# Second halves of a two-layer encoder kernel: attention steps four units apart, attends eight units behind, bias rows a pair ahead

## The reference

```python
def hybrid_layer(x, w_in, a_group_w, a_scale, b_sinks, c_rel_bias, w_out, ln_gain, ln_bias):
    h = jnp.einsum('bsd,de->bse', x, w_in)
    a_v, a_gate, b_q, b_k, b_v, b_gate, c_q, c_k, c_v, c_gate = jnp.split(h, _split_points(), axis=-1)
    a_out = pool_mixer(a_v, a_group_w, a_scale) * jax.nn.silu(a_gate)
    b_out = swa_sink_attention(b_q, b_k, b_v, b_sinks) * jax.nn.silu(b_gate)
    c_out = chunk_relbias_attention(c_q, c_k, c_v, c_rel_bias) * jax.nn.silu(c_gate)
    mix = jnp.concatenate([a_out, b_out, c_out], axis=-1)
    y = jnp.einsum('bse,ed->bsd', mix, w_out)
    return _layer_norm(DEEPNORM_ALPHA * x + y, ln_gain, ln_bias)
```

## Time and profile before

| what | before |
|---|---|
| median of three runs | 2870.41 us (2867.22 to 2871.13) |
| the profiled execution: time, span | 2874.22 us, 2872.4 us |
| PE busy | 2780.0 us, 97% of the span |
| DVE, ACT, POOL busy | 64%, 44%, 45% |
| low half of a unit on POOL (L1418), mean | 1410 ns |
| mean granted clock of TensorE | 0.989 |

### The profile page before, as it was taken

The page is one execution under the profiler, slowest core; times in us unless marked ns, Lnnn a source line. Parts: engine busy times, 40 slices in busy tenths (PEclk is TensorE's granted clock), DMA queues, the critical chain, the costliest instruction groups (busy, mean ns, idle before and its releaser), DMA issues.

```text
span 2872.4 us, 41015 instructions
## 1 busy us (share of the span) xinstructions
PE 2780.0 (97%) x12836; PEld 2313.4 (81%) x12836; DVE 1836.3 (64%) x2950; ACT 1267.9 (44%) x2612; POOL 1294.0 (45%) x927
## 2 busy tenths in 40 slices
PE   8888999999999999999999999999999999999998
PEld 7777888888877787888888888888888877788886
DVE  4555568732687777873157776796146778778624
ACT  4433456532344445553234444654234444456521
POOL 4334444444544444444454444444444444444441
PEclk9999999999999999999999999999999999999999
DMA  6555533255678873325567775323567667532442
GB/s 203 144 146 155 161 92 88 85 176 179 199 214 220 227 195 90 92 85 169 184 193 200 208 202 157 89 85 121 161 213 206 188 190 202 150 97 82 128 161 103
DMA packets 470981, 448.04 MB, mean 156 GB/s; under 512 B 257664, under 2 KB 308896, under 8 KB 467104
## 3 DMA queue, kind: packets, MB, share of 16 engines
q1 hardware_dynamic: 467024, 430.19, 52.1%
q10 hardware_dynamic: 3792, 15.73, 1.4%
HBM read 358.69 MB, written 90.27 MB: 156 GB/s over the span
## 4 chain that ended last, share of the span: by engine, by line
PE 78%; DVE 11%; DMA 6%; issue 2%; ACT 2%; SPq 1%; POOL 0%; ACTq 0%; POOLq 0%; DVEq 0%
PE acc L698 53%; PE sc L698 15%; PE pv L698 9%; DMA pt_raw<-c_prob_scratch 3%; DVE pt L1450 2%; DMA c_prob_scratch<-prob 2%; PE sc L767 1%; DVE mixl L1450 1%; DVE nmax L1504 1%; ACT pt L1030 1%; DVE c_att L1483 1%; DVE prob L1513 0%; DVE sc L1502 0%; DVE c_low L1480 0%; DVE b_keys L1450 0%
## 5 line engine op out<-in xcount | busy, mean ns | idle before, releaser
L1418 POOL TENSOR_TENSOR wl<-raw,wh 128x512 fp32r<-128x512 f32 x920 | 1293.2, 1410 | 1535.2 <-ACT wh L1030 1524.2
L1030 ACT ACTIVATE wh<-raw 128x512 fp32r<-128x512 f32 x920 | 574.0, 629 | 1071.7 <-PE acc L698 770.1
L698 PE MATMUL acc<-xh,wh 128*128 128x512 f32 x2624 | 1035.3, 395 | 7.5 <-DVE mixl L1450 4.1
L698 PE MATMUL acc<-xl,wh 128*128 128x512 f32 x2624 | 1027.5, 392 | 0.0
L698 PE MATMUL acc<-xh,wl 128*128 128x512 f32 x2624 | 1026.7, 391 | 0.0
L698 PEld LDWEIGHTS acc<-xh,wh 128*128 128x128 f32 x2624 | 496.8, 189 | 105.9 <-DVE mixl L1450 4.5
L698 PEld LDWEIGHTS acc<-xh,wl 128*128 128x128 f32 x2624 | 495.6, 189 | 106.6
L698 PEld LDWEIGHTS acc<-xl,wh 128*128 128x128 f32 x2624 | 496.5, 189 | 95.1
L1450 DVE TENSOR_TENSOR xl<-prob,xh 128x512 f32 x48 | 55.6, 1159 | 237.7 <-ACT xh L1030 237.7
L698 PE MATMUL sc<-wh,mixh 128*128 128x512 f32 x496 | 193.5, 390 | 0.1
L698 PE MATMUL sc<-wl,mixh 128*128 128x512 f32 x496 | 193.0, 389 | 0.0
(11 more groups left out here) (214 smaller groups left out, 3642.0 us busy)
## 6 DMA issues: line engine op xcount, KB each, us to landing
raw<-in_wall SPq DMA_DIRECT2D x920, 256.0 KB, 2.8
c_prob_scratch<-prob SPq DMA_DIRECT2D x128, 160.0 KB, 3.0
pt_raw<-c_prob_scratch SPq DMA_DIRECT2D x32, 640.0 KB, 5.1
res_scratch<-res ACTq DMA_DIRECT2D x12, 1024.0 KB, 4.3
res<-res_scratch SPq DMA_DIRECT2D x12, 1024.0 KB, 6.1
res<-in_x SPq DMA_DIRECT2D x8, 1024.0 KB, 6.9
x_scratch<-res SPq DMA_DIRECT2D x8, 1024.0 KB, 5.1
x_t_scratch<-turned SPq DMA_DIRECT2D x128, 64.0 KB, 2.7
```

The lines of the kernel that those rows point to most:

```text
L698: return nc.tensor.matmul(o, lhsT, rhs, start=start, stop=stop)
L1030: return nc.scalar.activation(o, i, ACT.Copy, scale=scale)
L1418: nc.gpsimd.tensor_tensor(wl[:, s, :], raw[:, s, :], wh[:, s, :].bitcast(F32), ALU.subtract).then_inc(w_lo, 1)
```

## The change

- Second halves get an order of their own on PE, ACT and DVE (`second_half`): scores after units 16, 20, 24 and 28, attends after 24, 28, 32 and 36 (24 is unit 0 of the next pair). SP stores and loads c_prob at u 26/28, 30/32, 34/36 and 38/40.
- In second halves the rows for gain and bias go to `brope[:, 0, :]` and `av` (`ln_rows`) and not to `prob`; they are loaded at s 22, store_ln and store_turned stand at u 27 to 31.
- `bias_rows` of pair p + 1 is issued by ACT in pair p behind slot 12, once bias_in of pair p has come; pair 0's stays.
- In it 0, `low_keys` stands ahead of the bias rows on DVE.
- Tails of all steps: B's second query tile is projected into `q_bank` (sc[1]); the B keys are split ahead of the last product of C; the transposed B values go to `vals` and not to `tmp`; b_scores waits for c_fold and not for the product. Pair 3 folds into `c_atts` and `c_lows` of other buffers.

```diff
-STORE_AT = (26, 29, 32, 36)
-LOAD_AT = (28, 31, 35, 38)
-ROPE_AT = C_PAIRS * 24 + 11
+STORE_AT = ((26, 29, 32, 36), (26, 30, 34, 38))
+LOAD_AT = ((28, 31, 35, 38), (28, 32, 36, 40))
+LAST_STORE_AT = (STORE_AT[0], (26, 30, 34, 36))
+LAST_LOAD_AT = (LOAD_AT[0], (28, 32, 35, 38))
+ROPE_AT = (C_PAIRS * 24 + 11, C_PAIRS * 24 + 12)
...
+        c_atts = [c_att] * (C_PAIRS - 1) + [av[:, 0:HALF]]
+        c_lows = [c_low] * (C_PAIRS - 1) + [res[:, 0, :]]
...
+        def ln_rows(it, slot):
+
+            if half(it + 1):
+                return (brope[:, 0, :], av[:, 0:HALF])[slot]
+            return prob[:, slot, 0:512]
...
+                if half(it + 1):
+                    sp.wait_ge(bias_ok, n + (C_PAIRS * (it + 1) + 2))
+                    sp.wait_ge(ay_ok, n + (C_PAIRS * (it + 1) + 1))
+                elif n:
                     sp.wait_ge(cp_out, 64 * c_step(it + 1, n, 0))
...
-                    if s == 10 and half(it):
+                    if s == (12 if half(it) else 10) and half(it):
...
-                    if s == 13 and it:
+                    if s == (22 if half(it) else 13) and it:
                         load_gain_bias(it - 1, p)
...
+                        if half(it) and u == q * U_C + 27:
+                            store_ln(it - 1, q)
+                        for t in range(QT):
+                            if half(it) and turns(it) and u == q * U_C + (27, 29, 29, 31)[t]:
+                                store_turned(it - 1, q, t)
...
-                pe.wait_ge(prod_ok, MIXES * it + 2 * C_PAIRS + 2)
+                pe.wait_ge(c_fold, 4 * C_PAIRS * (it + 1) + 2)
...
+                def second_half(p):
+                    def quarter(s, bank, **how):
+                        project(it, p * U_C + s, s % 4, acc[bank][:, :], s % RING, **how)
+
+                    if p:
+                        c_scores(it, p - 1, 2)
+                        c_attend(it, p - 1, 0)
+                    for s in range(1, 4):
+                        quarter(s, 0)
+                    pe.wait_ge(gate_ok, p * 2 + (MIXES * it + 1))
+                    pe.wait_ge(out_free, 16 * it + 8)
+                    quarter(4, 1)
+                    if p:
+                        c_scores(it, p - 1, 3)
+                        c_attend(it, p - 1, 1)
...
+                        if u in (KV0, KV0 + 2):
+                            c_scores(it, last, 2 + (u - KV0) // 2)
+                        if u in (KV0, KV0 + 4, KV0 + 7, B0 + 2):
+                            c_attend(it, last, (KV0, KV0 + 4, KV0 + 7, B0 + 2).index(u))
...
-                    def bias_rows():
+                    def bias_rows(q):
                         act.wait_ge(rel_out, 16)
+                        if q:
+                            act.wait_ge(bias_in, 16 * q)
...
                     slot(12)
+                    if it == 0 and p + 1 < C_PAIRS:
+                        bias_rows(p + 1)
...
```

The tail of DVE:

```diff
                 rotate(it, 1, KV0 + 7, 1, 1.0)
                 c_lo(it, p, 3)
-                c_add(it, p, 3)
-                c_tail_product(p, C_PAIRS * (it + 1))
-                dv.wait_ge(prod_ok, MIXES * it + 2 * C_PAIRS + 2)
...
-                mix_lo(nb + 2 * C_PAIRS, p + MIX_C)
                 if half(it):
                     dv.wait_ge(hist_mv, layer(it) + 1)
                 dv.wait_ge(qh_ok, ROTS * it + 2)
                 keys_lo([k[:, HD:] for k in bkl], s0[:, 0:HALF], [k[:, HD:] for k in bk]).then_inc(bq_ok, 1)
-                rotate(it, 2, B0 + 3, 0)
+                c_add(it, p, 3)
+                rotate(it, 2, B0 + 3, 1, source=q_bank)
+                c_tail_product(p, C_PAIRS * (it + 1))
+                dv.wait_ge(prod_ok, MIXES * it + 2 * C_PAIRS + 2)
                 rotated_query(ROTS * it + 3, 1)
+                dv.wait_ge(w_used, unit(it, B0 + 7) + (1 + RING))
+                V.transpose(vals, v_bank).then_inc(vt_ok, 1)
+                mix_lo(nb + 2 * C_PAIRS, p + MIX_C)
```

More of the change, by code:

```diff
@@ L600, in pair_end @@
                 def pair_end(p):
-                    if it:
+                    if it and not half(it):
                         if turns(it):
@@ L862, in _ @@
+                step(KV0)
+                for s in range(1, 4):
+                    project(it, KV0 + s, s, acc[0][:, :], s)
+                    step(KV0 + s)
                 pe.wait_ge(gate_ok, MIXES * it + 2 * C_PAIRS + 1)
@@ L1244, in _ @@
                 for p in range(C_PAIRS):
-                    pair(p, it + p == 0)
+                    if half(it):
+                        second_half(p)
+                    else:
+                        pair(p, it + p == 0)
                 last = C_PAIRS - 1
[L1248 to L1266, removed]
@@ L1655, in c_tail_product, with coefficients @@
                     dv.wait_ge(c_fold, c_step(it, p, 3) + 1 + 2)
-                    attention_product(p * 2 + (MIXES * it + 2), values)
-                for p in range(C_PAIRS):
-                    section(total)
-                    if p:
-                        c_max(it, p - 1, 3)
-                        c_lo(it, p - 1, 1)
+                    attention_product(p, p * 2 + (MIXES * it + 2), values)
+                def coefficients(p):
                     V.tensor_copy(coef1[:], coef[:, ds(p, 1), :].rearrange("p o n -> p (o n)"))
@@ L1670, in _, with pooling @@
                         V_(V.memset(av[:, 0:16], 0.0))
-                    if p:
-                        c_normalise(it, p - 1, 3)
-                        c_add(it, p - 1, 1)
-                        c_lo(it, p - 1, 2)
+                def pooling(p):
                     dv.wait_ge(av_ok, p + (pc + 1))
@@ L1756, in _ @@
                 p = C_PAIRS - 1
-                c_max(it, p, 3)
-                c_lo(it, p, 1)
-                c_normalise(it, p, 3)
-                c_add(it, p, 1)
-                c_lo(it, p, 2)
+                if half(it):
+                    for k in (*bk, *bkl):
+                        last = V.tensor_copy(k[:, 0:HD], k[:, HALF:HALF + HD])
+                    last.then_inc(hist_mv, 1)
+                    c_max(it, p, 2)
+                    c_add(it, p, 0)
+                    c_normalise(it, p, 2)
+                    c_lo(it, p, 1)
+                    c_max(it, p, 3)
+                    mix_lo(nb + 2 * C_PAIRS - 1, p + MIX_A)
+                    c_add(it, p, 1)
+                    c_normalise(it, p, 3)
+                    c_lo(it, p, 2)
+                else:
+                    c_max(it, p, 3)
+                    c_lo(it, p, 1)
+                    c_normalise(it, p, 3)
+                    c_add(it, p, 1)
+                    c_lo(it, p, 2)
                 dv.wait_ge(rope_in, 32 * (it + 1))
```

380 lines of the change are left out of this document (300 added, 80 removed).

## The result

The changed kernel takes **2930.3 us** (median of four runs, 2926.7 to 2932.1), the kernel before, run beside it, 2868.8 (2866.5 to 2871.1): ratio 1.0213, 95% interval 1.0195 to 1.0231, so 61.5 us slower. Predicted were 2848 us, and 2812 to 2871 as the range.

The account below looks back on a forecast made before the run. TensorE was taken as the bound, busy 97%, so only its idle time and slow clock could be won. Terms -27.5 + 6.6 - 4.8 + 0.9 + 2 = -22.8 us on 2874.2 gave 2851.4, as a median 2848; range 2812 to 2871.

Parts of the forecast that it names:

- bias rows: In it 0, issuing them a pair ahead removes three waits near 8 us and their slow clock: -27.5 us.
- attend 0, it 1, four pairs: PE's c_attend of step 0: SP stands at u 27 for turned rows, so load 0 is late, 3.3 us a pair.
- attend 1, it 1, three pairs: PE's c_attend of step 1: load_ln (1 MB) goes just ahead of its load, 0.4 us a pair.
- attend 3, it 1, three pairs: PE's c_attend of step 3: chain from attend 1's end 25.8 us, PE has 23.3, so 2.5 us late a pair.
- attend 3, it 3, three pairs: The same step 3 chain in the pairs of it 3: 2.5 us late a pair, bounds 0.3 and 6.7.
- tails: attend 2: PE's c_attend of step 2 in the tails of second halves: no wait counted, 0 us.
- tails: attend 3: Second halves' tails: c_lo 3 stands behind rotations and the rope load behind store 3, about 4.0 us late, twice.
- second halves, slow clock: Fewer waits, but seven above 3 us in it 1 and four in the tails: one more slow stretch, +2 us.
- Rival (2): Bias transfer only moves, holding history store and weights; PE waits 8 us in three pairs again: 2880 us, chance 0.08.
- the sizing of the second halves' waits: Late-step sums against the old waits: it 1 21.9 against 15.3, it 3 9.5 against 14.3, tails 12.6 against 11.7.
- Rival (3): Second halves' loads behind 1 MB take the upper bound, 6.7 us for 2.5, six times: 25 us more, 2873, chance 0.13.
- Rival (1): Second halves do as the spacing says: 29.6 us of waits and four slow stretches go, 2809 us, chance 0.20.

Follow-up runs that it names:

- e1: The kernel before with only the bias rows of pair p + 1 issued behind slot 12 of pair p: 2845.4 us, ratio 0.9913.
- e2: The changed kernel with the bias rows issued where the kernel before issues them: 2952.0 us, ratio 1.0283.
- e3: The changed kernel with SP's LN store at u 29 and turned rows at u 29, 29, 31, 31 in second halves: 2916.2 us, ratio 1.0156.
- e6: The changed kernel with second halves' load_ln moved to s 9 and history keys to s 13, behind loads 1 and 2 of c_prob: 2906.8 us, ratio 1.0126.
- e9: e8 with the second halves' turned rows moved on DVE from ahead of c_lo 0 to behind it: 2870.1 us, ratio 0.9996.
- e4: The changed kernel with c_normalise of step 3 ahead of c_lo of step 2 on DVE in second halves: 2882.4 us, ratio 1.0045.
- e8: The changed kernel with e3, e4, e6, ACT's splits of B0+4 and B0+5 ahead of the last mix_hi, and rope rows fetched at slot 11: 2841.1 us.
- e11: e8 with the wide spacing in it 3 alone, it 1 back in the order of the kernel before: 2832.6 us, ratio 0.9872.
- e10: e9 with the bias rows of the pair ahead issued behind slot 17 and not slot 12: 2874.2 us, ratio 1.0015.

## Why the prediction was wrong

By its own steps, predicted against the profile after:

| step | predicted | measured |
|---|---|---|
| bias rows | -27.5 | -26.0 (it 0's stretch); -25.2 alone (e1) |
| attend 0, it 1, four pairs | 3.3 each | 6.2, 7.0, 6.5, 5.7 |
| attend 1, it 1, three pairs | 0.4 each | 2.2, 2.0, 2.0 |
| attend 3, it 1, three pairs | 2.5 each | 5.8, 4.8, 5.8 |
| attend 3, it 3, three pairs | 2.5 each | 6.3, 6.8, 6.6 |
| attend 0, it 3, four pairs | 0.5 each | 0.5, 2.2, 2.0, 1.9 |
| tails: attend 2 | 0 | 3.6 twice |
| tails: attend 3 | 4.0 twice | 6.5, 6.1 |
| tails: B0+7 | 2.3 twice | 2.1, 1.7 |
| second halves, slow clock | +2 | +28.0 (20.7 and 7.3) |

**The bias rows** were right in mechanism and size, 23.7 us of waits against 23.8 of idle time (34.9 to 11.1); PE was 2.2 us less busy in it 0, where 5.8 were counted for the slow clock. A new stretch at 0.50 at 10.8 us (3.4 us) took back 1.7 of it, the rest stays open. Rival (2), the transfer that only moves, is out: e1 and e2. What pair 0 does (the wait stays, for `wl`) came as said.

**The step that failed is the sizing of the second halves' waits (+6.6 and -4.8, and +0.9 for the tails), and with it the clock term (+2).** The runs showed 42.4 us of waits in it 1 where it summed 21.9, 27.4 in it 3 where it summed 9.5, and 28.0 us of slow clock. Every wait that came was one that the prediction named, but for attend 2 in the tails and most of attend 1: it named the places and, in all, gave them 40% of their price. The waits came to 97.1 us (42.4 + 15.8 + 27.4 + 11.5) where it had summed 21.9 + 9.5 + 8 for attend 3 in the tails. Why:

- *Attend 0*: "SP stands at u 27 from 9 to 19.1" from the end of unit 16 (842.57) was from 14.1 to 21.4 in the trace, and load 0 went at 24.6, not 22.1, and took 5.59 us, not 4.9. The order's rule was right (e3 removes 14.0 us of it), DVE was 2.3 us later: gain alone takes 3.0.
- *Attend 1*: load_ln's 1 MB ahead of its load was named and priced at 0.4 us. e6, which moves it behind, takes the three waits of 2.0 to 2.2 us away whole. Turned rows stood ahead of load 1 too (four stores at 880.60, load 1 at 883.89), which the prediction didn't count; e9 shows what more of them cost.
- *Attend 3*: the sum 25.8 from attend 1's end is 28.4 in the trace (896.24 to 924.61). Load 2 (7.1, measured 7.2), load 3 (4.9, 5.1) and the copies fit; c_normalise took 3.9 and not 3.1, since one of DVE's two scalings ran 1.39 us for 0.55 (POOL, below), and from the first store to the load went 6.4 us, where 5.1 was summed: a unit's load and four issues of the values' store stand between. In it 3 load 2 took 7.8. What the prediction didn't do with this sum is ask why c_normalise 3 is in it at all: e4 takes it out, and 48 us with it. That is the largest part of the miss: the order was in the sum, at 2.5 us a pair.
- *Tails*: c_lo 3 behind the rope load was named; e8 shows that it cost attend 3 there, 11 us with its clock. Attend 2, put at nothing, waited 3.6 us twice and still waits 3.6 to 3.9 in e4 and e8; no run took that away.

**The clock.** The prediction took one more slow stretch for a dozen waits, +2 us. The rule that the rows gave (a stretch at 0.50 behind a wait of 7.8 us and, in the tail of it 1, behind one of 1.8; the 3.0 us there had none) was applied too sparingly: 19 stretches followed, some behind waits of 2.0 us.

The price of such a stretch can be read off the traces. PE's busy time, less half of what it was busy at 0.50, is 2759 to 2764 us in each of the thirteen kernels, while the busy time itself runs from 2772.6 (e11) to 2810.8 (e2). So half of PE's work at 0.50 is, within 5 us, all that the clock cost in any of them. The Trainium skill ("TensorE: Matmul & The Clock Gate", section "HAM oscillation — how this bites in real kernels") says that each wait for data that lets the clock fall makes PE start again at the low level, and that the penalty is the throttled time times 1 - 1.2/2.4. By that the 91.8 us more of such stretches (108.8 less 17.0) would cost 46 us; here PE's busy time rose by 28.0, because a stretch also holds the wait itself (10.20 us with 5.45 busy). The direction agrees, and so does the factor, once it is put to the part in which PE works.

Between the changed kernel and e11, PE's idle time falls by 71.0 us (128.0 to 57.0, span less busy) and the span by 100.7: each microsecond of wait taken away gave 1.4 us. It isn't a constant. From the kernel before to e1 it was 1.3, from the changed one to e4 1.4 and to e6 1.5, from e8 to e9 1.6; but from e9 to e10 PE idles 8.6 us more in short waits, is 6.1 us less busy, and the span grows by 2.5 only.

Rival (3), loads behind 1 MB at their upper bound, came nearest of the rivals (6.7 a pair of it 3, measured 6.3 to 6.8; 2873 in all), but by another sum: the load of step 2 took 6.4 to 8.4 us in the six pairs and not 11.3, the rest was order on DVE and SP, and its sign was met by attend 3 alone, not by attend 2. Rival (1), that the spacing works as it says, is true only of a kernel with five other orders changed, and then it is worth 9 us in it 3 and a loss in it 1. What stays open is attend 2 in the tails.

Two smaller questions the traces answer. In e8 attend 1 of pair 0 in it 1 waits 3.8 us where that of pair 1 waits 0.2: load 1 goes 8.9 us after attend 0 (in pair 1 8.0), takes 5.5 us to land (4.4), and PE has no stretch at 0.50 between the two, which in pair 1 (3.4 us) puts off the need by 1.7. And the same scaling of DVE takes 0.55 or 1.39 us by what POOL does. The one at 906.40 ends at 907.79, 0.35 us after this one of POOL:

```profile
905.80 1.64 POOL L1628 TENSOR_TENSOR wl<-raw,wh 128x512 fp32r<-128x512 f32 x1 [1.43 <-ACT wh L1122]
```

In the thirteen traces all 258 scalings of 128x640 that took 1.25 to 1.69 us end 0.35 to 0.36 us after the end of a `wl` of POOL that began before them or within 0.04 us of them; the 574 others took 0.55 to 0.59, and no `wl` that ran when they began went on for more than 0.24.

## What to carry to other kernels

When a chain is given more room (units between its steps), look at each in-order queue for the instruction that stands behind a wait it doesn't need: here two lines of DVE (an idle of 6.81 us at the head, ready work behind it) cost 48 us, and the LayerNorm's and the turned stores at the wrong unit of SP's program 14. Add a chain up with the rows of its neighbours and then add a margin, since here nearly every term turned out larger than summed: a forecast that finds the waits and gives them 40% of their size can have the wrong sign. On an engine that is 97% busy a wait costs more than its length: 1.3 to 1.6 times here where waits of 2 us and more went, a good deal less where only short ones came (e10).

## What of the hardware was not expected

- Waits of 2.0 us were followed by 3.4 us at a granted clock of 0.50 (the 1.2 GHz level), while none of the waits of 1.0 to 1.4 us in it 2 was, nor one of 2.0 us in it 3. Over the thirteen traces, the first 20 us of each left out, 1 of 118 waits of 0.9 to 1.7 us of PE had such a stretch at it (running when the wait ended, or begun within 1.8 us of that), 34 of 67 of 1.8 to 2.4, 29 of 34 of 2.7 to 3.6 and all 96 longer ones.
- The same load of 640 KB took 4.3 to 9.4 us from issue to landing in the changed kernel. The twelve right behind two transfers of 512 KB or one of 1 MB took 6.4 to 9.4, eighteen of the twenty others 5.9 at most, and moving the large ones behind it (e6) was worth 23.6 us.
- A scaling on DVE that begins while POOL writes a `wl` takes up to 1.69 us for 0.55, and ends 0.35 us after POOL does.
